# A two-layer expert stage on one core: routing chain overlapped, the stop before the block loop taken out, and block 0's rows gathered apart from the pairs

## What is computed

```python
def hier_moe(xf, w_rg, b_rg, w_re, b_re, w1, w3, w2):
    g_prob = jax.nn.softmax(xr @ w_rg + b_rg, axis=-1)
    g_val, g_idx = lax.top_k(g_prob, 1)
    e_in = ...                       # logits of the 8 experts of that group
    top_v, top_i = lax.top_k(e_in, 2)
    gate = jax.nn.softmax(top_v, axis=-1) * g_val
    ...                              # rows sorted by expert, each expert padded to whole blocks
    def expert_block(args):
        xblk, e = args
        return (jax.nn.silu(xblk @ w1[e]) * (xblk @ w3[e])) @ w2[e]
```

## Time and profile before

| | |
|---|---|
| median of 3 runs | 3084.39 us (3083.84 to 3085.94) |
| the profiled execution, its own time | 3084.61 us |
| its span in the trace | 3082.8 us |
| PE busy | 2763.1 us, 90% |
| DVE, ACT, POOL busy | 1293.5, 805.2, 270.0 us |
| moved by DMA | 666.06 MB, 216 GB/s over the span |
| granted TensorE clock, mean | 0.946 of full speed |

### The profile page before, as it was taken

One profiled execution on the slowest core, in us unless ns is written; L12 is line 12 of the kernel. 1 busy time (PEld: TensorE's weight loads), 2 busy tenths in 40 slices (PEclk: granted clock), 3 DMA queues, 4 the chain that ended last, 5 costly groups with the idle time before them and its releaser, 6 DMA issues. The chain is left out here.

```text
span 3082.8 us, 34488 instructions
## 1 busy us (share of the span) xinstructions
PE 2763.1 (90%) x12578; PEld 1809.7 (59%) x12578; DVE 1293.5 (42%) x2007; ACT 805.2 (26%) x1339; POOL 270.0 (9%) x390
## 2 busy tenths in 40 slices
PE   7999989999989999799959988886888978998886
PEld 5888867766767888587833433333655543433333
DVE  5776685555457675603241110112556641111012
ACT  3223235454343232322220000001326620000000
POOL 0111100000001111021100111110000000111110
PEclk9999999999999999899979999998898988999997
DMA  5565521211225666311078999988110058999997
GB/s 207 212 220 219 211 89 69 70 68 69 103 88 185 219 220 237 137 68 41 28 288 360 422 387 393 404 346 331 47 43 1 1 234 349 421 370 399 401 401 286
DMA packets 116868, 666.06 MB, mean 216 GB/s; under 512 B 16158, under 2 KB 20638, under 8 KB 52128
## 3 DMA queue, kind: packets, MB, share of 16 engines
q1 hardware_dynamic: 77024, 536.35, 44.4%
q0 software_dynamic: 33408, 104.90, 9.7%
q10 hardware_dynamic: 6336, 23.50, 2.1%
HBM read 685.38 MB, written 24.38 MB: 230 GB/s over the span
## 5 line engine op out<-in xcount | busy, mean ns | idle before, releaser
L917 PE MATMUL bank<-big 128*64 128x512 f32 x784 | 361.8, 608 | 67.4 <-DMA big<-in_w 65.3
L2256 DVE TENSOR_TENSOR big<-big,bank 64x512 f32<-64x512 f32 x65 | 45.0, 692 | 845.0 <-ACT big L1504 845.0
L920 PE MATMUL bank<-big 128*64 128x512 f32 x848 | 392.0, 608 | 0.0
L917 PEld LDWEIGHTS bank<-big 128*64 128x64 f32 x784 | 105.2, 140 | 299.0 <-issue 297.0
L932 PE MATMUL bank<-big 128*64 128x512 f32 x912 | 243.5, 683 | 29.5 <-DVE big L2260 29.5
L1927 DVE SCALAR_TENSOR_TENSOR tabs<-tabs,tmp 128x1024 f32<-128x1024 f32 x160 | 193.6, 1223 | 178.4 <-DMA tabs<-in_wm 177.8
L1357 ACT ACTIVATE w_high<-slot 128x1024 fp32r<-128x1024 f32 (+1 forms) x138 | 140.8, 1041 | 205.2 <-DMA slot<-in_w 103.3
L2673 POOL DMA_DIRECT2D tabs<-in_wm x160 | 85.0, 532 | 1164.4 <-DVE tabs L1927 724.4
L607 PE MATMUL bank<-u_split,w_low 128*128 128x512 f32 x720 | 177.8, 389 | 0.0
L1504 ACT ACTIVATE big<-bank 64x512 f32<-64x512 f32 x65 | 38.3, 589 | 491.9 <-PE bank L917 491.9
L932 PEld LDWEIGHTS bank<-big 128*64 128x64 f32 x912 | 68.8, 155 | 161.7 <-issue 124.4
(11 more groups left out here) (408 smaller groups left out, 5323.3 us busy)
## 6 DMA issues: line engine op xcount, KB each, us to landing
big<-in_w SPq DMA_DIRECT2D x330, 1024.0 KB, 16.1
slot<-in_w SPq DMA_DIRECT2D x120, 1024.0 KB, 4.8
tabs<-in_wm POOLq DMA_DIRECT2D x160, 512.0 KB, 4.8
ar_u<-in_w SPq DMA_DIRECT2D x24, 1024.0 KB, 14.6
slot<-in_wd SPq DMA_DIRECT2D x16, 1408.0 KB, 6.6
ar_f<-in_w SPq DMA_DIRECT2D x20, 1024.0 KB
tabs<-in_w SPq DMA_DIRECT2D x10, 1024.0 KB
tmp<-in_w SPq DMA_DIRECT2D x10, 1024.0 KB
```

The costliest lines, as they stand in the source:

```text
L917: ga = nc.tensor.matmul(bank[0][lo, :], xT[:, 4 * c + k, :], w1[:, k * EF:(k + 1) * EF], **flags)
L920: mm = nc.tensor.matmul(bank[0][hi, :], xT[:, 4 * c + k, :], w3[:, k * EF:(k + 1) * EF], **flags)
L2256: nc.vector.tensor_tensor(hmul[MB:2 * MB, :], hsil[MB:2 * MB, :], bank[0][MB:2 * MB, :], ALU.mult).then_inc(q["h_ready"], 1)
```

## The change

1. The wait for the expert row is taken out of the middle of the routing chain: DVE goes straight to the ranks, and writes `exp_i` after the one-hot matrices. PE makes the expert row behind the first of the table's matmuls.
2. The products with the two choices are made in one operation of twice the width (`picked`, `choices`).
3. Each pair of one-hot matrices releases PE by itself, and PE multiplies it at once.
4. `phase.end()` before the loop becomes a wait for `expert` on each engine.
5. `EARLY_ROWS` is 4, with a fourth row buffer.
6. SP loads 7 of the 12 guessed parts of layer 0 before the last dense part ends, and 2 of 12 in layer 1. The last two parts of block 2 wait for the first gather to land.
7. `gather_first` fetches the 64 rows of block 0 alone; pair m now holds blocks 2m - 1 and 2m, and waits for `xt_full >= 2 * m - 1`. `gather(rotated)` goes, since pair 6 holds blocks 11 and 12.

```diff
-        EARLY_ROWS = 3
+        EARLY_ROWS = 4
...
                 if l == 0:
+                    sp.wait_ge(xc_ready, 2 * KT + 4)
+                    for c in ORDER[3:]:
+                        load(c, NE - 1)
+                    sp.wait_ge(dft_full, 4)
+                    for c in ORDER[1:2] + ORDER[3:]:
+                        load(c, NE - 2, 1)
                     sp.wait_ge(full[3], R_EO + 4)
+                    for c in ORDER[:3]:
+                        load(c, NE - 1)
+                    for c in (0, 1):
+                        load(c, NE - 2, 1)
...
                 sp.wait_ge(q["table"], l + 1)
+                sp.wait_ge(q["gathered"], 16)
                 for c in ORDER[4:]:
                     load(c, e2, 2)
...
-                pe.wait_ge(q["routed"], routed(l, "tab_in"))
-                for x in range(2 * nt):
-                    mm = nc.tensor.matmul(bank[2][:, 0:TABW], at_place[:, x, :], in_block[:, x, :],
-                                          start=(x == 0), stop=(x == 2 * nt - 1))
+                for n in range(2 * nt):
+                    pe.wait_ge(q["routed"], placed(l, n + 1))
+                    mm = nc.tensor.matmul(bank[2][:, 0:TABW], at_place[:, n, :], in_block[:, n, :], start=(n == 0), stop=(n == 2 * nt - 1))
+                    if n == 0:
+                        nc.tensor.matmul(bank[6][0:2, 64:64 + TABW], ones[0:NE, 0:2], cmpb[0:NE, 0:TABW], start=True,
+                                         stop=True).then_inc(q["route_sums"], 1)
...
-                phase.end()
+                pe.wait_ge(q["expert"], l + 1)
...
-                    spread_x(b + 1, (b + 1) // 2 if b + 1 < rotated else None)
+                    spread_x(b + 1, b // 2 + 1)
...
-                nc.vector.tensor_tensor(tab_u[MB:P, 0:TABW - 1], used[MB:P, 1:TABW], tab_f[MB:P, 1:TABW], ALU.add)
+                nc.vector.tensor_tensor(tab_u[MB:P, 1:TABW], used[MB:P, 0:TABW - 1], tab_f[MB:P, 0:TABW - 1], ALU.add)
...
+                def gather_first():
+                    pool.indirect_dma_start(out=xg[0:MB, :], out_offset=None, in_=d["rows"][l],
+                                            in_offset=bass.IndirectOffsetOnAxis(ap=tab_u[0:MB, 0:1], axis=0),
+                                            bounds_check=SC - 1, oob_is_err=False).then_inc(q["gathered"], 16)
+
                 def gather_pair(m):
-                    if m > 0:
-                        pool.wait_ge(q["xt_full"], 2 * m)
+                    pool.wait_ge(q["xt_full"], 2 * m - 1)
...
-                gather_pair(0)
-                phase.end()
+                gather_first()
+                pool.wait_ge(q["expert"], l + 1)
                 last = pool.value_load(exp_i[0:1, TABW:TABW + 1], min_val=rotated + 3, max_val=NBMAX - 1)
-                for m in range(1, rotated // 2):
+                for m in range(1, rotated // 2 + 1):
                     gather_pair(m)
                     scatter_early(2 * m - 2)
-                    scatter_early(2 * m - 1)
-                gather(rotated)
-                scatter_early(rotated - 2)
+                    if m < rotated // 2:
+                        scatter_early(2 * m - 1)
```

More of the change, by code:

```diff
@@ L278, in program @@
         yrows = [[part((2 * t + x) * D, [D]) for x in range(2)] for t in range(TT)]
-        row_bufs = [xg] + [part(third_at + n * D, [D]) for n in range(2)]
+        row_bufs = [xg] + [part(third_at + n * D, [D]) for n in range(2)] + [part(m0 + D, [D])]
         rt = third_at + 2 * D
@@ L287, in program @@
         oh = [part(rt + 648 + 192 * n, [TT, NE]) for n in range(2)]
+        choices = part(rt + 648, [2, TT, NE])
         both = part(rt + 1032, [TT, NE])
+        picked = part(rt + 1032, [2, TT, NE])
         rank = part(rt + 1224, [TT, NE])
@@ L1510, in copy_y @@
                     nc.scalar.activation(ysb, bank[4][:, :], ACT.Copy).then_inc(q["y_ready"], 1)
-                phase.end()
+                act.wait_ge(q["expert"], l + 1)
                 last = act.value_load(exp_i[0:1, TABW:TABW + 1], min_val=2, max_val=NBMAX - 1)
@@ L2186, in moe_layer @@
                 dve.drain().then_inc(q["routed"], 1)
[L2188 to L2196, removed]
                 dve.wait_ge(q["route_sums"], route_sum(l, "ranks"))
@@ L2209, in moe_layer @@
                 nc.vector.tensor_copy(ovv, ovi)
-                dve.drain()
+                dve.wait_ge(q["route_sums"], route_sum(l, "starts"))
                 nc.vector.tensor_copy(nbb[:, 0:NE], bank[5][:, 0:NE])
+                nc.vector.tensor_copy(col[0:NE, 2:3], bank[6][0:NE, 0:1])
                 dve.drain()
@@ L2216, in moe_layer @@
                 nc.vector.scalar_tensor_tensor(elv, start, float(MB), rkv, ALU.mult, ALU.add)
-                dve.drain()
+                nc.vector.tensor_scalar(cmpb[0:NE, 0:TABW], const("count")[0:NE, 0:TABW], col[0:NE, 2:3], None, ALU.is_lt)
+                dve.drain().then_inc(q["routed"], 1)
                 for which, src in ((0, elv), (1, ecv)):
[L2219 to L2222, removed]
+                    nc.vector.tensor_tensor(picked[:, :, 0:nt, :], choices[:, :, 0:nt, :],
+                                            src.unsqueeze(1).to_broadcast([P, 2, nt, NE]), ALU.mult)
+                    dve.drain()
+                    over_last(pos_f[:, which, :, 0:nt], picked[:, :, 0:nt, :], ALU.add)
                 dve.drain()
@@ L2227, in moe_layer @@
                 dve.drain()
+                dve.wait_ge(q["xt_cp"], TT * l + min(nt, EARLY_ROWS + 1))
+                if nt == EARLY_ROWS:
+                    dve.wait_ge(q["xt_out"], 16 * (TT * l + nt))
                 for t in range(nt):
                     for x in range(2):
+                        nc.vector.tensor_scalar(in_block[:, 2 * t + x, :], const("count")[:, 0:TABW], pos_f[:, 1, x, t:t + 1],
+                                                const("tok")[:, x * TT + t:x * TT + t + 1], ALU.is_equal, ALU.mult)
                         nc.vector.tensor_scalar(at_place[:, 2 * t + x, :].rearrange("p (n r) -> p n r", n=2),
                                                 const("spread").unsqueeze(1).to_broadcast([P, 2, MB]), place[:, x, t:t + 1], None,
-                                                ALU.is_equal)
-                        nc.vector.tensor_scalar(in_block[:, 2 * t + x, :], const("count")[:, 0:TABW], pos_f[:, 1, x, t:t + 1],
-                                                const("tok")[:, x * TT + t:x * TT + t + 1], ALU.is_equal, ALU.mult)
-                dve.drain().then_inc(q["routed"], 1)
+                                                ALU.is_equal).then_inc(q["routed"], 1)
+                dve.wait_ge(q["route_sums"], route_sum(l, "exp_row"))
+                nc.vector.tensor_scalar(exp_i[0:1, 0:TABW], bank[6][0:1, 64:64 + TABW], -1.0, 0.0, ALU.add, ALU.max)
+                nc.vector.tensor_scalar(exp_i[0:1, TABW:TABW + 1], bank[7][0:1, TABW:TABW + 1], -1.0, None, ALU.add)
+                dve.drain().then_inc(q["expert"], 1)
                 dve.wait_ge(q["route_sums"], route_sum(l, "tab_full"))
@@ L2260, in copy_h @@
                     nc.vector.tensor_copy(hT, bank[6][:, 0:EF // P * MB]).then_inc(q["ht_ready"], 1)
-                phase.end()
+                dve.wait_ge(q["expert"], l + 1)
                 last = dve.value_load(exp_i[0:1, TABW:TABW + 1], min_val=2, max_val=NBMAX - 1)
```

21 lines of the change are left out of this document (11 added, 10 removed).

## The result

The changed kernel takes 3128.85 us (median of 4 runs, 3128.39 to 3131.51) against 3084.11 us for the kernel before on the same chip (4 runs, 3083.69 to 3085.94). The ratio is 1.0145, with a 95% interval of 1.0133 to 1.0158: 44.7 us slower. The forecast was 3130 us, in a range of 3102 to 3150.

What follows compares the result with a forecast made beforehand. A layer's stage was taken as block 0's start, plus 12 blocks paced by PE, plus an untouched tail. 3084.6 - 16.1 (earlier starts) + 62 (late pairs) = 3130.5, forecast 3130 us, range 3102 to 3150.

Steps and rivals of the forecast that it cites:

- Term 1: Chain before block 0, first gather included: gain of 9.6 us in layer 0, net 6.5 in layer 1, together 16.1.
- the detour: Routing chain, layer 0: DVE goes to the ranks without waiting for the expert row, gaining 2.1 us.
- the products: Routing chain, layer 0: four products and four sums done at twice the width in four steps, gaining 0.95 us.
- the table: Routing chain, layer 0: matmuls started behind the first one-hot pair instead of after all 12, gaining 4.3 us.
- Term 2: Block loop: pairs behind a scatter awaiting a result come late, five a layer, 6.2 us each, 62 us loss.
- the middle: Wait of PE for a late pair: 4.8 us, between 4.0 and 5.6, because the scatter ahead shares its transfer time.
- The price of the drop: Granted clock on PE after each late pair's wait: a drop to the 1.2 GHz level costing 1.4 us.
- The moves at nothing: Stop before the loop, late release of `expert`, guessed loads moved ahead: zero, with 1 us possible in layer 1.
- The tail behind block 12: Blocks on one weight set at the end of a layer's stage: the change does not touch their time.
- Late `expert`: Start of the stage: `expert` released some 9 us later, block 2's first loads near 1606 instead of 1599.31; zero cost.
- The pair lands in time: Block loop: a pair lands within 4.2 us of issue, no waits, 3068.5 us; chance 0.08.
- Longer: Block loop: pair's descriptors made only after the scatter moved, landing 11 us or more after issue, 3152 us; chance 0.13.

Runs made afterwards that it cites:

- experiment 8: The kernel of experiment 1 with EARLY_ROWS back at 3 and three row buffers; 3063.84 us.
- experiment 5: The kernel of experiment 1 with the expert row made and released before the one-hot pairs, so the weights go out earlier; 3066.5 us.
- experiment 6: The kernel before, with SP holding block 2's loads until the first gather of 128 rows has landed; 3076.35 us.
- experiment 3: The changed kernel with the pairs as before (blocks 0 and 1 first, 128 rows, old loop on GpSimd); 3062.47 us.
- experiment 2: The kernel before with the new pairing alone (first gather of 64 rows, pairs from block 1 on, new GpSimd loop); 3147.91 us.
- experiment 1: The changed kernel with each pair's gather issued ahead of the scatter of the block before, waiting only for its buffer; 3064.1 us.
- experiment 9: The kernel of experiment 1 with `phase.end()` back in place of the wait for `expert` on four engines; 3064.18 us.
- experiment 7: The kernel of experiment 1 with SP's guessed loads issued where the kernel before has them; 3061.92 us.
- experiment 4: The changed kernel with each pair still held for the result of the block before, but issued ahead of the scatter; 3113.39 us.

## Why the prediction was right, and its errors in size

- **Term 1, up to the gather's issue.** Forecast 7.4 us in layer 0 (9.6 less 2.2 for the gather), measured 7.1: the detour 2.1, the products 0.9, the table 4.2 (forecast 2.1, 0.95 and 4.3). The table's part rests on the fourth row, which the prediction priced only as a cost: with three rows (experiment 8) the chain gains 4.4 us, not 7.1. In layer 1 DVE's part was forecast at 5.7 us and is 5.5 (13.72 from ACT's exp to the gather against 19.20 in the earlier trace rows). Against it stands the fourth row on ACT: forecast 1.2, measured 1.8 (9.6 us from the logits to the exp before, 11.4 after; 9.5 with three rows in experiment 8). Layer 1's net is thus 3.7 us, forecast 4.5.
- **Term 1, the gather: the wrong step.** It was taken as 7.5 us, "what a scatter of the same bytes takes", a row from a full stream. It took 3.2 us, so this piece gave 6.5 and 6.4 us, not 2.2 and 2.0. The prediction had in hand that SP's loads would go out late and priced that at nothing; experiments 5, 6 and 8 show that this is what makes the gather quick. The halved row count, which the prediction credited, gives 0.8 us (3.2 us for 64 rows, 4.0 for 128 in experiment 3), and beside the weights 0.7 and 1.0 us (experiment 2). Term 1 came out at 23.6 us, forecast 16.1 and outside its bound of 20.
- **A rule and the trace.** The Trainium skill, "DMA: Bandwidth & Descriptors", section "Anatomy of one DMA — SWDGE (gpsimd) path", gives 2.0 us plus bytes at 436 GB/s: an estimate of 2.6 us for 64 rows of 4 KB and 3.2 for 128. On idle DMA engines the runs have 3.1 to 3.3 us and 3.3 to 4.2, somewhat above it; beside the weights they have 6.3 to 9.9 us, and no row there agrees.
- **Term 2.** Five late pairs in each layer, at blocks 3, 5, 7, 9 and 11: as forecast. The wait was forecast at 4.8 us and is 5.6 in layer 0 and 4.5 in layer 1. The rest was forecast at 1.4 us for each pair; it is 1.4 in layer 0 ((34.8 - 27.8) / 5) and 2.0 in layer 1 ((32.8 - 22.6) / 5). The 1.4 is net of a spacing of 14.9 us that the kernel before has once in layer 0, from block 3 to 4, with its clock at 0.50 for some 3 us and no long wait; counted against 13.51 us a block, a late pair costs 1.7 us there beside its wait. Together 67.6 us, forecast 62. In layer 0 the pair took 9.6 us from issue to PE, 0.6 more than the 9.0 assumed (4.2 + 4.8), which is near the upper end of the bound, the first gather of the earlier trace rows, rather than the middle that was taken; and POOL issued it 2.8 us behind ACT's copy, not 2.5. The reason given for the middle, that the scatter ahead shares the pair's transfer time, is not borne out: experiment 1's pairs are as slow without it. The price of the drop was read from block 13, which has a drop of some 3 us and no such wait; block 14, which had the wait, lost 6.28 - 4.1 = 2.2 us beside it. Behind a late pair the granted clock is 0.50 for the first 6.8 us of work (window at 1650 us). That the rest is the clock is argued from this window, not shown by a run of its own.
- **The errors cancel.** 7.5 us too little gain and 5.6 us too little loss leave the sum 1.9 us off, so the closeness of 3130 to 3128.85 is partly luck.
- **The moves at nothing.** The stop and the guessed loads: confirmed in the time, within the spread of the runs (experiments 9 and 7). Behind a gather this quick the stop no longer hides, though: it is 1.0 us at the start of each layer. The tail behind block 12: 340.0 us before, 340.2 after. DMA's idle stretch before block 13: there. Late `expert`: not neutral, as above.
- **The rivals.** "The pair lands in time" failed as a forecast of this kernel, but its price was near: 3068.5 us with no late pair, against 3064.1 when experiment 1 issues it in time. "Longer", with descriptors made only after the scatter has moved and 11 us or more for a pair, is refuted: the pair for blocks 3 and 4 needs 9.6 us with the scatter just ahead, and 9.0 (experiment 4) or some 9.9 to land (experiment 1) without.

## What to carry to other kernels

In an in-order queue a transfer's issue time is the release of everything that stands ahead of it: before its buffer or its size, ask what the instruction ahead waits for. When a fetch is moved to start one consumer later, as here from block 0 to block 1, move its place in the queue too; the order that was harmless before cost 63 to 65 us (experiments 2 and 1). And a small transfer on a critical path is worth clearing the DMA engines for: weights that set out 2 us behind a gather instead of with it made it some 5 us shorter, though a stream that is itself the bound later takes part of that back.

## What the hardware showed unexpectedly

- **Idle engines halve a small gather.** From issue on POOL to landing, both layers: 3.1 to 3.3 us for 64 rows of 4 KB and 3.3 to 4.2 us for 128 rows, when the weights are issued 2 us or more later (the kernel after, experiments 1, 3 and 6); 8.3 us for 64 rows when they are issued 0.1 us later (experiment 8), 7.8 and 6.8 us when they are on their way (experiment 5), 7.9 to 9.9 us for 128 rows in the middle of the stage (experiments 1 and 3). Beside the stream, half the rows saved 0.7 and 1.0 us (experiment 2).
- **A pair of rows is as slow with no scatter near it** (8.1 to 9.9 us in layer 0 of experiment 1) **as with one issued 1.3 us ahead in the same queue** (9.3 to 9.8 us in the kernel after). What the scatter ahead costs for certain is its issue, 1.3 us.
- A start 8 us later in layer 0 cost 3 us at its end. An engine's lead on a saturated stream is worth less than it looks.
